# Second block of a transformer kernel: both heads of a pair in one attention unit, rotation by DMA instead of a matmul

## The chip, the cores and the metric

The kernel runs on one core of one Trainium2 chip. The metric is the device time of one execution in microseconds. Three runs of the kernel before gave 2832.24, 2833.23 and 2835.91 us; the median is 2833.23.

## What is computed

A first block of two layers (feed forward, a mixer with pooling, a Fourier part and differential attention, feed forward) and a second block of two layers. The change touches the second block alone:

```python
def hybrid_layer(x, mem, norm_g, w_in, w_out, mem_norm_g, w_mem_kv, qk_g):   # T = 512, D = 1024
    proj = rms_norm(x, norm_g) @ w_in
    a_q, a_k, a_v, a_g, b_q, b_k, b_v, b_g, m_q, m_g = split(proj)           # 6 + 6 + 4 heads of 64
    qa, ka = rope(rms_norm(heads(a_q), qk_g[0])), rope(rms_norm(heads(a_k), qk_g[1]))
    oa = moba_attention(qa, ka, heads(a_v))          # causal: T = 512 is two blocks, all of them kept
    qb, kb = rope(rms_norm(heads(b_q), qk_g[2])), rope(rms_norm(heads(b_k), qk_g[3]))
    ob = dilated_attention(qb, kb, heads(b_v))       # one softmax with a mask of log counts
    m_k, m_v = split(rms_norm(mem, mem_norm_g) @ w_mem_kv)                   # 256 memory rows
    om = memory_attention(rms_norm(heads(m_q), qk_g[4]), rms_norm(m_k, qk_g[5]), m_v)
    y = concat([oa * silu(a_g), ob * silu(b_g), om * silu(m_g)])
    return x + y @ w_out
```

rope turns a head's halves x1, x2 of 32 rows into x1 cos - x2 sin and x2 cos + x1 sin.

## The kernel before

**Precision.** Each float32 product is made of three matmuls of split operands (hi times hi, hi times lo, lo times hi), by `three` (L414 to L420). A weight panel is 128 x 2048 numbers: SyncE loads it into one of two raw buffers, ScalarE copies it to w_hi (`split`, two instructions of 1024 columns, L840), GpSimd subtracts the rest into w_lo (L410, four of 512 columns). Activations lie feature-major, features on partitions, the 512 tokens along the row.

**Groups.** A layer of the second block has eight groups. Group 0 is the memory's keys and values, group 1 the memory queries and gates, groups 2 to 7 one pair of heads each, with four chunks: queries, keys, values, gate. A chunk is 8 x 3 matmuls of 128 x 512, half of it 12.

**Stages.** `run_stages` goes through the layer in stages, and in each the attention of one group stands beside the projection (`producer`) of the next. The memory stage has 16 steps, every second one with half a chunk. Each pair stage has 8 steps with half a chunk each: five with a producer (groups 2 to 6 attend, 3 to 7 are projected), and a last one (group 7) beside which the output projection begins (`beside_last`, then `tail` and `project_out`).

**A unit** is one head and one block of 128 queries; its width is 256 for memory, and 128, 256, 384, 512 keys for blocks 0 to 3 of a pair. In step s each engine runs, in this order written by hand (`attention_step`):
- TensorE: scores of unit s (three matmuls on the 64 rows of the head, bank s % 2); transposes of unit s - 3 by the identity (L705, bank 2 + s % 2); after each fourth unit, a step later, the outputs of that head (`outputs`, in bank 5); in step 5 the transposes of the values (L717); then the producer's part: in steps 2 and 4 first the rotation and the mean of squares as plain float32 matmuls (L730, L731), then half a chunk in bank 4 (the gate in bank 7).
- VectorE: mask and maximum of unit s (L1452), negation; in step 7 the split of the next pair's queries and keys (qk_hi, qk_lo, L1438 and L1187 in `head_split`); scaling of unit s - 1 by the reciprocal sum (att, L1473); remainder of the transposed unit s - 3 (pt_lo); the gate product; the producer's part: in steps 3 and 5 mean and rotation (L1515 to L1528), in step 6 value, Newton steps and scaling (L1531, L1180, L1182, L1432).
- ScalarE: first the producer's part (copy and square of the chunk, L1029 and L1030, steps 2 and 4, and in step 4 a weight split); exp of unit s (L1056); copy of the transposed unit s - 3 (pt_hi, L1065); in step 5 the guesses of the reciprocal roots (L858), in step 7 a weight split and the gate's Silu (L1045). Silu, exp and root each load their table.

Engines are joined by counting semaphores: t_scores, t_max, t_exp, t_att, t_tr, t_thi, t_tlo for the links of a unit, t_o and t_y for outputs, hn_in, hn_mm, hn_ms, hn_rot, hn_guess, hn_out for queries and keys. TensorE starts a pair stage only after hn_out, that is, after qk_lo.

Of the kernel before, what the change touches and what calls it, by code (L numbers as in the profile page):

```python
# [71 lines left out]
C_ID, C_MEAN, C_HALF, C_HEAD, C_ROT = range(5)  # L72
NC = 5 * P + 1
# [22 lines left out]
UNITS2 = 64  # L96
PAIR_UNITS = 2 * TB


class Stage:  # L100
# [3 lines left out]
    def __init__(self, l, gi, branch):  # L104
        self.l, self.gi, self.branch = l, gi, branch
        self.memory = branch is None
        self.last = isinstance(gi, int) and gi == GROUPS - 1
        if self.memory:
            self.n, self.widths = 4 * TB, [256] * (4 * TB)
            self.u0, self.heads0 = UNITS2 * l, 16 * l  # L110
        else:
            self.n, self.widths = PAIR_UNITS, [P * (b + 1) for _ in range(2) for b in range(TB)]
            self.u0 = UNITS2 * l + 4 * TB + PAIR_UNITS * (gi - 2)
            self.heads0 = 16 * l + 4 + 2 * (gi - 2)
# [4 lines left out]
LAG_TR = 3  # L119
LAG_OUT = 4  # L120
LAG_GATE = 5
# [5 lines left out]
def lagged(here, before, s, lag):  # L127

    i = s - lag
    if i < 0:  # L130
        return (before, before.n + i) if before else None
    return (here, i) if here and i < here.n else None


def run_stages(l, fori, step, producer, last=None, tail=None):


    def stage(here, before, produce):
        for s in range(here.n if here else LAG_GATE + 1):
            if here and here.memory:  # L140
                step(here, before, s, produce, s // 2 if s % 2 == 0 else None)
            else:
                step(here, before, s, produce, s)
    memory = Stage(l, 1, None)
    stage(memory, None, producer(l, 2))
    pair = Stage(l, 2, 0)
    stage(pair, memory, producer(l, 3))
    for first, branch in ((3, 0), (5, 1)):
        with fori(0, 2) as j:
            pair = Stage(l, first + j, branch)  # L150
            stage(pair, Stage(l, first - 1 + j, branch), producer(l, first + 1 + j))
    pair = Stage(l, 7, 1)
    stage(pair, Stage(l, 6, 1), last)
    stage(None, pair, tail)


def shape_constants():
# [7 lines left out]
    rot = np.zeros((P, P))  # L165
    for m in range(P):
        if m % 64 < 32:
            rot[m + 32, m] = -1.0
        else:
            rot[m - 32, m] = 1.0  # L170
    consts[:, C_ROT * P:(C_ROT + 1) * P] = rot
# [14 lines left out]
    rope = np.stack([np.cos(ang).T[i % 32], np.sin(ang).T[i % 32]], 1)  # L186
# [18 lines left out]
def build(nc, x, mem, stream, vecs1, vecs2, final_g, lamv, consts, dist, masks, recip, rope, out):  # L205
    ctx = ExitStack()
    with ctx:  # L207
# [78 lines left out]
        vm_hi = sb("vm_hi", [P, 2, 2, 2, P], F32R, two)  # L286
        vm_lo = sb("vm_lo", [P, 2, 2, 2, P], F32R, two)
# [3 lines left out]
        pt_hi = sb("pt_hi", [P, TB, T], F32R, two)  # L291
        pt_lo = sb("pt_lo", [P, TB, T], F32R, two)
        rope_sb = sb("rope_sb", [P, 2, T], F32, two)
        mask = sb("mask", [P, 2, T], F32, two)
        prob2 = sb("prob2", [P, 2, T], F32, two)
        att2 = sb("att2", [P, 2, T], F32, two)
        xs = sb("xs", [P, 2, T], F32, two)
        qk_hi = sb("qk_hi", [P, 2, T], F32R, two)
        qk_lo = sb("qk_lo", [P, 2, T], F32R, two)
        two.close()  # L300
        mh_hi = pt_hi[:].rearrange("p a (b n) -> p (a b) n", b=2)
        mh_lo = pt_lo[:].rearrange("p a (b n) -> p (a b) n", b=2)
# [61 lines left out]
        hn_rot = sem("hn_rot")  # L364
        hn_guess = sem("hn_guess")
# [49 lines left out]
        def _(pe):  # L415
# [245 lines left out]

            def scores(stage, u):
                h, b = u // TB, u % TB
                r, c, w = slice(64 * (h % 2), 64 * (h % 2) + 64), slice(P * b, P * b + P), slice(0, stage.widths[u])
                if stage.memory:
                    k_split = km_hi[r, h // 2, w], km_lo[r, h // 2, w]
                else:
                    k_split = qk_hi[r, 1, w], qk_lo[r, 1, w]
                return three(ps[:, u % 2, w], qk_hi[r, h // 2, c], qk_lo[r, h // 2, c], *k_split, True, True)

            def outputs(stage, h):
                l, gi = stage.l, stage.gi
                if stage.memory:
                    if h == 2:
                        pe.wait_ge(t_y, 8 * l + 1)
                    for kb in range(2):
                        mm = three(ps[:, 5, :], vm_hi[:, kb, h // 2, h % 2, :], vm_lo[:, kb, h // 2, h % 2, :],
                                   pt_hi[:, kb, :], pt_lo[:, kb, :],
                                   h % 2 == 0 and kb == 0, h % 2 == 1 and kb == 1)
                else:  # L680
                    if h == 0:
                        pe.wait_ge(v_tlo, 7 * l + gi)
                    for kb in range(TB):
                        c = slice(P * kb, T)
                        mm = three(ps[:, 5, c], vp_hi[:, kb, h, :], vp_lo[:, kb, h, :],
                                   pt_hi[:, kb, c], pt_lo[:, kb, c],
                                   h == 0 and kb == 0, h == 1 and kb == TB - 1)
                mm.then_inc(t_o, 1)

            def attention_step(here, before, s, produce, part):  # L690
                if here:
                    if s == 0 and not here.memory:
                        pe.wait_ge(hn_out, GROUPS * here.l + here.gi + 1)
                    unit2 = lagged(here, before, s, 2)
                    if unit2:
                        pe.wait_ge(t_exp if unit2[0].memory else t_max, here.u0 + s - 1)
                    scores(here, s).then_inc(t_scores, 1)
                unit = lagged(here, before, s, LAG_TR)
                if unit:
                    stage, u = unit  # L700
                    pe.wait_ge(t_att, stage.u0 + u + 1)
                    if u >= 2 or not stage.memory:
                        pe.wait_ge(t_tlo, stage.u0 + u - 1)
                    for kb in range(stage.widths[u] // P):
                        mm = pe.transpose(ps[:, 2 + u % 2, P * kb:P * kb + P],  # L705
                                          att2[:, u % 2, P * kb:P * kb + P], const(C_ID))
                    mm.then_inc(t_tr, 1)
                unit = lagged(here, before, s, LAG_OUT)
                if unit and unit[1] % TB == TB - 1:
                    stage, u = unit  # L710
                    pe.wait_ge(t_tlo, stage.u0 + u + 1)
                    outputs(stage, u // TB)
                if here and not here.memory and s == 5:
                    pe.wait_ge(v_in, 7 * here.l + here.gi)
                    pe.wait_ge(t_y, 8 * here.l + here.gi)
# [4 lines left out]
                if produce and part is not None:  # L720
                    produce(part)

            def producer(l, gi):
# [3 lines left out]
                rot0 = 12 * l + 2 * (gi - 2)  # L727

                def rotate(j):
                    pe.matmul(ps[:, 6, :], const(C_ROT), xs[:, j, :], start=True, stop=True)  # L730
                    pe.matmul(ps[:, 7, :], const(C_HALF), sq[:, j, :], start=True, stop=True).then_inc(hn_mm, 1)  # L731

                def step(s):
                    if s > 7:
                        return
# [20 lines left out]
                    if s % 2:  # L756
                        mm.then_inc(panel_done if c % 2 else chunk_ready, 1)
                return step

            def stack2(l):  # L760
# [44 lines left out]
                def beside_last(s):  # L805
# [8 lines left out]
                run_stages(l, pe.Fori, attention_step, producer, beside_last, tail)  # L814
                project_out(p0 + 2 * GROUPS, 0, lambda i: pe.wait_ge(y_ready, 8 * l + i + 1), Y_ORDER,
                            (KB - 1, PAIR_UNITS - 2, 0, 0))
# [17 lines left out]
        def _(act):  # L834
# [212 lines left out]
            def attention_step(here, before, s, produce, part):  # L1047
                if produce and part is not None:
                    produce(part)
# [3 lines left out]
                if here:  # L1053
                    w = slice(0, here.widths[s])
                    act.wait_ge(t_max, here.u0 + s + 1)
                    act.activation(prob2[:, s % 2, w], ps[:, s % 2, w] if here.memory else prob2[:, s % 2, w],  # L1056
                                   ACT.Exp, bias=nmx[:, s % 2, 0:1], accum_out=ssum[:, s % 2, 0:1]).then_inc(t_exp, 1)
                unit = lagged(here, before, s, LAG_TR)
                if unit:
# [679 lines left out]
```

## Time and profile before

| | |
|---|---|
| three runs | 2832.24, 2833.23, 2835.91 us |
| profiled execution, its own time | 2830.71 us |
| its span | 2828.9 us |
| TensorE matmuls busy | 2607.4 us (92%) |
| VectorE busy | 1319.6 us (47%) |
| ScalarE busy | 1083.6 us (38%) |
| GpSimd busy | 1109.1 us (39%) |
| granted TensorE clock, mean | 0.957 |

A busy time is the sum over an engine's instructions; matmuls overlap their neighbours, so the length of one (0.39 us) is more than its distance to the next (0.23 us). Idle time in brackets in a row is the time before the instruction, and the arrow names what ended it. The second block takes the last 27% of the span.

### The profile page before, as it was taken

The numbers are of one execution on the slowest core, as the hardware profiler recorded it, in microseconds if no ns is written. First come the engines' busy times: TensorE is split into PE (matmuls) and PEld (weight loads), VectorE is DVE, ScalarE is ACT, GpSimd is POOL, SyncE is SP. The second block draws the span as 40 slices with busy tenths as digits, with TensorE's granted clock in tenths as the row PEclk, the third lists the DMA queues.
The fourth block names the chain that finished last, engine by engine and source line by source line (L and its number), as shares of the span: only waits on it lengthen the run. The fifth ranks groups of instructions, "written<-read, shape, count | busy, mean of one in ns | idle before, by whom it ended". The sixth has DMA issues, their size and how long they took to land.

```text
span 2828.9 us, 32377 instructions
## 1 busy us (share of the span) xinstructions
PE 2607.4 (92%) x11338; PEld 2055.2 (73%) x11338; DVE 1319.6 (47%) x2355; ACT 1083.6 (38%) x1594; POOL 1109.1 (39%) x828
## 2 busy tenths in 40 slices
PE   6999999679999999999997799999989997889988
PEld 5887887457887888878874578878756665756656
DVE  5544034645443044440346454430856666556563
ACT  4333133534332143331335343321545442545442
POOL 3544445214544445544452145454512222412222
PEclk9999999789999999999997899999989998999989
DMA  4222233102222222222331022223201111201111
GB/s 154 90 101 92 89 110 113 45 29 91 89 104 89 90 91 102 96 97 90 105 117 45 27 93 89 103 90 120 104 30 60 45 45 45 90 30 46 59 45 60
DMA packets 32858, 226.94 MB, mean 80 GB/s; under 512 B 4096, under 2 KB 4096, under 8 KB 6016
## 3 DMA queue, kind: packets, MB, share of 16 engines
q1 hardware_dynamic: 30816, 218.12, 21.6%
q10 hardware_dynamic: 1952, 7.61, 0.7%
q8 instruction: 58, 0.95, 0.1%
q14 instruction: 32, 0.26, 0.0%
HBM read 223.62 MB, written 2.10 MB: 80 GB/s over the span
## 4 chain that ended last, share of the span: by engine, by line
issue 63%; POOL 37%; POOLq 1%
POOL w_lo L410 37%; POOLq L404 0%; POOLq L408 0%; POOLq L207 0%; POOLq L410 0%; POOLq L1730 0%
## 5 line engine op out<-in xcount | busy, mean ns | idle before, releaser
L410 POOL TENSOR_TENSOR w_lo<-raw,w_hi 128x512 fp32r<-128x512 f32 x824 | 1108.9, 1377 | 1719.3 <-ACT w_hi L840 1718.9
L418 PE MATMUL ps<-h_hi,w_hi 128*128 128x512 f32 x2304 | 937.2, 407 | 32.0 <-POOL w_lo L410 11.2
L419 PE MATMUL ps<-h_lo,w_hi 128*128 128x512 f32 x2304 | 910.0, 395 | 0.0
L420 PE MATMUL ps<-h_hi,w_lo 128*128 128x512 f32 x2304 | 909.7, 395 | 0.0
L840 ACT ACTIVATE w_hi<-raw 128x1024 fp32r<-128x1024 f32 x412 | 413.3, 1052 | 827.6 <-PE ps L420 819.7
L418 PEld LDWEIGHTS ps<-h_hi,w_hi 128*128 128x128 f32 x2304 | 441.1, 191 | 136.0 <-issue 29.5
L419 PEld LDWEIGHTS ps<-h_lo,w_hi 128*128 128x128 f32 x2304 | 441.4, 192 | 97.7 <-issue 9.5
L420 PEld LDWEIGHTS ps<-h_hi,w_lo 128*128 128x128 f32 x2304 | 440.3, 191 | 95.2
L418 PE MATMUL ps<-hid_hi,w_hi 128*128 128x512 f32 x704 | 279.7, 397 | 7.5 <-DVE hid_lo L1187 7.5
L420 PE MATMUL ps<-hid_hi,w_lo 128*128 128x512 f32 x704 | 278.6, 396 | 0.0
L419 PE MATMUL ps<-hid_lo,w_hi 128*128 128x512 f32 x704 | 278.3, 395 | 0.0
L1240 DVE SCALAR_TENSOR_TENSOR x_sb<-ps,x_sb 128x512 f32<-128x512 f32 x64 | 43.7, 687 | 438.7 <-PE ps L420 438.7
L1259 DVE TENSOR_TENSOR sq<-hraw,sq 128x512 f32<-128x512 f32 x88 | 139.7, 1588 | 222.6 <-ACT hraw L927 222.6
L840 ACT ACT_TABLE_LOAD x42 | 53.9, 1283 | 320.2 <-PE ps L420 315.7
L418 PEld LDWEIGHTS ps<-hid_hi,w_hi 128*128 128x128 f32 x704 | 132.6, 188 | 41.1 <-DVE hid_lo L1187 9.2
L1255 DVE TENSOR_TENSOR hraw<-ps,guess 128x512 f32<-128x512 f32 x88 | 60.8, 691 | 213.2 <-PE ps L420 212.4
L420 PEld LDWEIGHTS ps<-hid_hi,w_lo 128*128 128x128 f32 x704 | 132.6, 188 | 32.9
L419 PEld LDWEIGHTS ps<-hid_lo,w_hi 128*128 128x128 f32 x704 | 132.4, 188 | 31.6
L1056 ACT ACTIVATE prob<-prob,nmx 128x128 f32<-128x128 f32 (+1 forms) x96 | 54.0, 563 | 204.4 <-DVE nmx L1456 204.0
L1187 DVE TENSOR_TENSOR pt_lo<-ps,pt_hi 128x256 fp32r<-128x256 f32 (+3 forms) x128 | 60.6, 474 | 127.6 <-ACT pt_hi L1065 127.6
L1261 DVE CAST hid_hi<-sq 128x512 f32 (+1 forms) x88 | 111.2, 1264 | 14.7 <-issue 14.5
L1187 DVE TENSOR_TENSOR hid_lo<-sq,hid_hi 128x512 f32 (+1 forms) x88 | 100.6, 1143 | 12.6 <-issue 0.2
(261 smaller groups left out, 2669.6 us busy)
## 6 DMA issues: line engine op xcount, KB each, us to landing
raw<-in_stream SPq DMA_DIRECT2D x206, 1024.0 KB, 4.9
x_sb<-in_x ACTq DMA_DIRECT2D x1, 2048.0 KB, 10.6
out_x<-x_sb SPq DMA_DIRECT2D x8, 256.0 KB, 2.7
mem_sb<-in_mem ACTq DMA_DIRECT2D x1, 1024.0 KB, 13.5
rec_sb<-in_recip ACTq DMA_DIRECT2D x2, 512.0 KB, 4.8
memn<-in_mem ACTq DMA_DIRECT2D x1, 1024.0 KB, 4.9
dist_sb<-in_dist ACTq DMA_DIRECT2D x2, 448.0 KB, 3.8
mask<-in_masks ACTq DMA_DIRECT2D x1, 512.0 KB, 5.9
```

The source lines that it names most:

```text
L410: ins = gp.tensor_tensor(w_lo[:, s, c], raw[:, s, c], w_hi[:, s, c].bitcast(F32), ALU.subtract)
L418: pe.matmul(dst, l_hi, r_hi, start=first, stop=False)
L419: pe.matmul(dst, l_hi, r_lo, start=False, stop=False)
L420: return pe.matmul(dst, l_lo, r_hi, start=False, stop=last)
L840: act.activation(w_hi[:, s, c], raw[:, s, c], ACT.Copy).then_inc(hi_split, 1)
L1056: act.activation(prob2[:, s % 2, w], ps[:, s % 2, w] if here.memory else prob2[:, s % 2, w], ACT.Exp, bias=nmx[:, s % 2, 0:1], accum_out=s ...
L1187: return dve.tensor_tensor(dst, src, hi.bitcast(F32), ALU.subtract)
L1240: dve.scalar_tensor_tensor(out=x_sb[:, m, :], in0=ps[:, m, :], scalar=scale, in1=x_sb[:, m, :], op0=ALU.mult, op1=ALU.add).then_inc(x_read ...
L1255: dve.tensor_tensor(hraw[:, e, :], ps[:, 2 * e, :], rstd, ALU.mult).then_inc(gate_in, 1)
L1259: dve.tensor_tensor(sq[:, e, :], hraw[:, e, :], sq[:, e, :], ALU.mult)
L1261: dve.tensor_copy(hid_hi[:, c, :], sq[:, e:e + 1, :])
```

## The change

`UNITS2` falls from 64 to 32 a layer. A unit is now both heads of a pair and one query block: the memory group has 8, each pair 4, and all stages have 8 steps, pair stages a unit in every second one (`every = 2`), written out without loops. Scores go by `paired`, head 0 to bank 0 and head 1 to bank 1, interleaved; the transposes of a pair unit fill banks 2 and 3, prob2 and att2 hold one unit. The lags are 1 for the scaling, 2 for the transposes, 3 for the outputs (both heads at once), 4 for the gate product. The rotation matmul is gone: ScalarE's queue issues four DMAs of 32 partitions that write xs, with its halves exchanged, to hraw, and the sign lies in the table. The mean matmul stands behind the half-chunk. The final-norm products of x_sb go to the odd steps of stages 2 and 3.

```diff
-LAG_TR = 3
-LAG_OUT = 4
-LAG_GATE = 5
+LAG_ATT = 1
+LAG_TR = 2
+LAG_OUT = 3
+LAG_Y = 4
...
+            def paired(dst, l_hi, l_lo, r_hi, r_lo, first, last):
+
+                for a, b, f, z in ((l_hi, r_hi, first, False), (l_hi, r_lo, False, False), (l_lo, r_hi, False, last)):
+                    for h in range(2):
+                        mm = pe.matmul(dst[h], a[h], b[h], start=f, stop=z)
+                return mm
...
+                    if u and stage.memory:
+                        pe.wait_ge(t_exp, stage.u0 + u)
+                    elif not stage.memory:
+                        pe.wait_ge(t_exp if u == 0 and before.memory else t_max, stage.u0 + u)
+                    scores(stage, u).then_inc(t_scores, 1)
+                unit = lagged(here, before, s, LAG_OUT)
+                if unit and ends_group(unit[1]):
+                    stage, u = unit
+                    pe.wait_ge(t_tlo, stage.u0 + u + 1)
...
-                    pe.matmul(ps[:, 6, :], const(C_ROT), xs[:, j, :], start=True, stop=True)
...
+                def turn(j):
+
+                    g = v2_all[:, bass.ds(NV2 * l + G_QK + 2 * gi + j, 1)]
+                    act.activation(xs[:, j, :], ps[:, 4, :], ACT.Copy, scale=g).then_inc(xs_ready, 1)
+                    act.activation(sq[:, j, :], ps[:, 4, :], ACT.Square).then_inc(hn_in, 1)
+                    act.wait_ge(xs_ready, rot0 + j + 1)
+                    if j == 1:
+                        act.wait_ge(hn_rot, rot0 + 1)
+                    for i in range(4):
+                        o, n = 32 * i, 32 * (i ^ 1)
+                        act.dma_start(hraw[o:o + 32, 1, :], xs[n:n + 32, j, :]).then_inc(turned, 16)
...
+                        dve.wait_ge(turned, 64 * (12 * l + 2 * (gi - 2) + j + 1))
                         dve.tensor_tensor(xs[:, j, :], xs[:, j, :], rope_sb[:, 0, :], ALU.mult)
-                        dve.tensor_tensor(hraw[:, 1, :], ps[:, 6, :], rope_sb[:, 1, :], ALU.mult)
+                        dve.tensor_tensor(hraw[:, 1, :], hraw[:, 1, :], rope_sb[:, 1, :], ALU.mult)
```

ScalarE in a pair stage, from step 4 to the end of step 7: xs and sq are copy and square of the keys, prob the exp, pt_hi the copy of the transposes, w_hi a weight split. Before:

```order
L1029 ACTIVATE xs<-ps,v_all 128x512
L1030 ACTIVATE sq<-ps 128x512
L837 ISA
L840 ACTIVATE w_hi<-raw 128x1024 x2
L1055 REGISTER_ALU
L1056 ACTIVATE prob,ssum<-prob,nmx 128x128
L1065 ACTIVATE pt_hi<-ps 128x2x128
```

In the changed kernel, the same place:

```order
L1113 ACTIVATE xs<-ps,v_all 128x512
L1114 ACTIVATE sq<-ps 128x512
L1120 DMA hraw<-xs 32x512 x4
L852 ACTIVATE w_hi<-raw 128x1024 x2
L1075 ACTIVATE prob,ssum<-prob,nmx 128x384 x2
L1089 ACTIVATE pt_hi<-ps 128x2x2x128
```

Four DMA issues now stand between the square and the weight split, and the exp and the copy behind it are those of two heads and of wider blocks.

VectorE at the end of a pair stage, steps 6 and 7: mx and nmx are the maximum, hraw the value, newt and guess the Newton steps. Before:

```order
L1187 TENSOR_TENSOR pt_lo<-ps,pt_hi 128x4x128
L1531 TENSOR_TENSOR hraw<-ps,scale 128x512
L1180 SCALAR_TENSOR_TENSOR newt<-ms,newt 128x1024
L1182 SCALAR_TENSOR_TENSOR guess<-newt,guess 128x1024
L1432 SCALAR_TENSOR_TENSOR xs<-xs,guess 128x512 x2
L1445 REGISTER_ALU
L1451 MEMSET tick 128x1
L1452 ISA prob,mx<-ps,mask 128x512
L1452 ISA mx 128x1
L1456 TENSOR_SCALAR nmx<-mx 128x1
L1438 CAST qk_hi<-xs 128x1024
L1187 TENSOR_TENSOR qk_lo<-xs,qk_hi 128x1024
```

In the changed kernel:

```order
L1490 ISA prob,mx<-ps,mask 128x512
L1490 ISA mx 128x1
L1493 TENSOR_SCALAR nmx<-mx 128x2
L1223 TENSOR_TENSOR pt_lo<-ps,pt_hi 128x2x3x128
L1569 TENSOR_TENSOR hraw<-ps,scale 128x512
L1216 SCALAR_TENSOR_TENSOR newt<-ms,newt 128x1024
L1218 SCALAR_TENSOR_TENSOR guess<-newt,guess 128x1024
L1468 SCALAR_TENSOR_TENSOR xs<-xs,guess 128x512 x2
L1474 CAST qk_hi<-xs 128x1024
L1223 TENSOR_TENSOR qk_lo<-xs,qk_hi 128x1024
L1511 RECIPROCAL rsum<-ssum 128x2
L1514 TENSOR_SCALAR att<-prob,rsum 128x512 x2
```

The maximum of the widest block moved from between xs and the split to ahead of the remainder, which is that of two heads; no unit stands in step 7.

## Rows read from the trace of the kernel before

**Rows 1.** Stretches: start:end, length, busy us (count) of each engine, clock, DMA.

```profile
2050.90:2114.75 63.85, 52.93 (x197) 35.83 (x197) 38.92 (x100) 24.52 (x57) 8.23 (x7) 0.85 0.09 33
2114.75:2336.96 222.21, 203.84 (x872) 147.49 (x871) 135.76 (x375) 112.88 (x208) 51.30 (x40) 0.96 0.13 48
2336.96:2385.96 49.00, 41.38 (x171) 30.77 (x172) 29.07 (x86) 14.21 (x34) 5.25 (x4) 0.79 0.06 22
2464.57:2523.03 58.46, 48.77 (x196) 33.49 (x196) 33.18 (x92) 24.52 (x57) 7.79 (x7) 0.91 0.10 37
2523.03:2743.70 220.67, 201.84 (x872) 145.45 (x872) 135.72 (x375) 112.78 (x208) 51.33 (x40) 0.97 0.13 48
2743.70:2791.05 47.35, 39.86 (x171) 29.70 (x172) 28.80 (x85) 14.10 (x34) 5.27 (x4) 0.82 0.06 23
```

**Rows 2.** Waits of TensorE from 2114 us on: us in total, times, longest.

```profile
PE ps L418 <- DVE qk_lo L1187: 26.8, 10, 3.1
```

**Rows 3.** First block's scores by tile k_hi, 552 to 554 us: ns, first and last start.

```profile
L418 PE MATMUL ps<-k_hi,q_hi x2: 791/792/792, 552.2 to 552.3; 64*128 64x512 f32 x2
```

**Rows 4.** TensorE in order of time, pair stage from 2159 us: start, length, line, operation.

```profile
2167.90 1.13 PE L730 MATMUL ps<-xs,cst 128*128 128x512 f32 x2
2168.86 1.02 PE L731 MATMUL ps<-sq,cst 128*128 128x512 f32 x2
...
2172.57 0.50 PE L418 MATMUL ps<-qk_hi 64*128 64x512 f32 x1
...
2173.55 0.48 PE L418 MATMUL ps<-pt_hi,vp_hi 128*128 128x512 f32 x1
...
2175.49 0.45 PE L418 MATMUL ps<-h_hi,w_hi 128*128 128x512 f32 x1
...
2178.41 0.33 PE L418 MATMUL ps<-qk_hi 64*128 64x128 f32 x1
```

**Rows 5.** VectorE in order of time, end of the same stage.

```profile
2188.75 0.68 DVE L1525 TENSOR_TENSOR xs<-xs,rope_sb 128x512 f32<-128x512 f32 x1
...
2190.72 0.55 DVE L1452 CUSTOM_DVE_ANT_0 prob<-ps,mask 128x384 f32<-128x384 f32 x1
...
2193.59 0.69 DVE L1187 TENSOR_TENSOR pt_lo<-ps,pt_hi 128x512 fp32r<-128x512 f32 x1 [1.54 <-ACT pt_hi L1065]
...
2198.98 0.69 DVE L1452 CUSTOM_DVE_ANT_0 prob<-ps,mask 128x512 f32<-128x512 f32 x1
...
2199.82 0.68 DVE L1438 CAST qk_hi<-xs 128x1024 fp32r<-128x1024 f32 x1
...
2201.96 1.47 DVE L1473 TENSOR_SCALAR att<-prob,rsum 128x384 f32<-128x384 f32 x1
```

**Rows 6.** ScalarE in order of time, the same stage.

```profile
2161.43 0.63 ACT L1045 ACTIVATE y<-y 128x512 f32<-128x512 f32 x1 [0.15 <-DVE y L1510]
2162.09 1.28 ACT L1056 ACT_TABLE_LOAD   x1
...
2178.62 0.69 ACT L1029 ACTIVATE xs<-ps,v_all 128x512 f32<-128x512 f32 x1 [2.65 <-PE ps L420]
...
2179.68 2.00 ACT L840 ACTIVATE w_hi<-raw 128x1024 fp32r<-128x1024 f32 x2
...
2192.37 0.62 ACT L1056 ACTIVATE prob<-prob,nmx 128x384 f32<-128x384 f32 x1
2192.99 0.58 ACT L1065 ACTIVATE pt_hi<-ps 128x512 fp32r<-128x512 f32 x1
```

**Rows 7.** A DMA issue on ScalarE's queue, and DMA issues by line: us to landing.

```profile
1973.07 0.45 ACTq L946 DMA_DIRECT2D mask<-in_masks  x1
...
out_x<-x_sb SPq DMA_DIRECT2D x8, 256.0 KB, 2.7
```

**Rows 8.** VectorE by tile: ns least, median, most; sq in the first block, qk_lo.

```profile
L1259 DVE TENSOR_TENSOR sq<-hraw,sq x88: 1476/1667/1823, 43.7 to 1883.5; 128x512 f32<-128x512 f32 x88
...
L1187 DVE TENSOR_TENSOR qk_lo<-xs,qk_hi x14: 1224/1225/2129, 2048.0 to 2742.4; 128x1024 fp32r<-128x1024 f32 x14
```

More of the change, by code:

```diff
@@ L129, in lagged, with ends_group, run_stages @@
     i = s - lag
[L130 to L154, printed above, removed]
+    stage = here if i >= 0 else before
+    i %= STEPS
+    if stage is None or s - lag >= STEPS or i % stage.every:
+        return None
+    return stage, i // stage.every
+def ends_group(u):
+    return u % TB == TB - 1
+def run_stages(l, step, producer, last=None, tail=None):
+    before = None
+    for gi in range(1, GROUPS):
+        here = Stage(l, gi, None if gi == 1 else (gi - 2) // 3)
+        produce = producer(l, gi + 1) if gi + 1 < GROUPS else last
+        for s in range(STEPS):
+            step(here, before, s, produce)
+        before = here
+    for s in range(LAG_Y):
+        step(None, before, s, tail)
 def shape_constants():
@@ L290, in build @@
         km_lo = sb("km_lo", [P, 2, 256], F32R, two)
[L291 to L296, printed above, removed]
+        pt_hi = sb("pt_hi", [P, 2, TB, T], F32R, two)
+        pt_lo = sb("pt_lo", [P, 2, TB, T], F32R, two)
         xs = sb("xs", [P, 2, T], F32, two)
@@ L665, in scores @@
                 if stage.memory:
-                    k_split = km_hi[r, h // 2, w], km_lo[r, h // 2, w]
-                else:
[L668 to L688, printed above, removed]
@@ L690, in attention_step @@
-            def attention_step(here, before, s, produce, part):
-                if here:
+                    q, k = [[t[r, u // TB, c] for r in rows] for t in (mq_hi, mq_lo)], (km_hi, km_lo)
+                    k = [[t[r, u // TB, w] for r in rows] for t in k]
+                else:
+                    q = [[t[r, 0, c] for r in rows] for t in (qk_hi, qk_lo)]
+                    k = [[t[r, 1, w] for r in rows] for t in (qk_hi, qk_lo)]
+                return paired([ps[:, h, w] for h in range(2)], *q, *k, True, True)
@@ new lines, in outputs @@
+            def outputs(stage, u):
+                kbs = 2 if stage.memory else TB
+                for h in range(2):
+                    for kb in range(kbs):
+                        if stage.memory:
+                            c, v = slice(0, T), (vm_hi[:, kb, u // TB, h, :], vm_lo[:, kb, u // TB, h, :])
+                        else:
+                            c, v = slice(P * kb, T), (vp_hi[:, kb, h, :], vp_lo[:, kb, h, :])
+                        mm = three(ps[:, 5, c], *v, pt_hi[:, h, kb, c], pt_lo[:, h, kb, c],
+                                   h == 0 and kb == 0, h == 1 and kb == kbs - 1)
+                return mm
@@ L692, in attention_step @@
+            def attention_step(here, before, s, produce):
+                unit = lagged(here, before, s, 0)
+                if unit:
+                    stage, u = unit
                     if s == 0 and not here.memory:
                         pe.wait_ge(hn_out, GROUPS * here.l + here.gi + 1)
[L694 to L697, printed above, removed]
+                    if u and stage.memory:
[5 more added lines that the diff above has]
+                if unit and ends_group(unit[1]):
+                    stage, u = unit
+                    pe.wait_ge(t_tlo, stage.u0 + u + 1)
+                    if not stage.memory:
+                        pe.wait_ge(v_tlo, 7 * stage.l + stage.gi)
+                    elif u >= TB:
+                        pe.wait_ge(t_y, stage.outs0 + 1)
+                    outputs(stage, u).then_inc(t_o, 1)
@@ L719, in attention_step @@
                     mm.then_inc(v_tr, 1)
-                if produce and part is not None:
-                    produce(part)
+                if produce:
+                    produce(s)
             def producer(l, gi):
```

248 lines of the change are left out of this document (134 added, 114 removed).

## The prediction

> **What bounds the kernel now.** I read the time by stage first, because the change only touches the two attention layers at the end [rows 1]. A layer's memory stage takes 63.85 and 58.46 us, its five pair stages with a producer take 222.21 and 220.67 us (44.3 each), and the last pair stage with the start of the output projection 49.00 and 47.35 us. In the five stages TensorE is busy 204 of 222 us: these are bound by TensorE. What it waits for is small and always the same: 26.8 us in ten waits for VectorE's qk_lo [rows 2], once a stage, when the next pair's queries and keys are not yet split. So two questions decide: how much TensorE work goes, and whether VectorE and ScalarE can follow when TensorE asks sooner. In the memory stage TensorE already idles (52.9 of 63.9 us), so there only the waits count.
>
> **TensorE work that goes.** The rotation matmul costs 0.96 us (2167.90 to 2168.86) [rows 4], twice a stage: 1.9 us. The scores of the two heads of a pair lie on different row halves. In the first block the program has three matmuls for one half and then three for the other, and the first matmuls of both halves start within 0.1 us of each other, with equal durations [rows 3]: the halves run at once. A pair of score units then costs what one costs now: 0.98 us at width 512 with its hand-over (2172.57 to 2173.55) [rows 4], and by columns some 0.5, 0.6, 0.8 for the narrower ones. Four of eight units and their hand-overs from and to the 128-row matmuls go: 3.3 us a stage, as an estimate. Together 5.2 of some 40 us a stage, 52 us over ten stages: that is the offer. Nothing else shrinks: four half-chunks and four more (2.75 each, 2.92 with hand-over), outputs 1.94 a head, means 0.9 [rows 4].
>
> **What the change puts in their place.** Scores use banks 0 and 1 for one unit, transposes banks 2 and 3 for one unit, prob2 and att2 hold one unit. Every link of softmax is now twice as long and the distance from scores to transposes falls from three steps to two. And rotation issues eight DMAs a stage on ScalarE's queue: one there took 0.45 us [rows 7], so some 1.7 us for four. What stands behind them on ScalarE, the weight split and the next exp, starts only then. Landing, 2.7 us for the nearest row, out_x [rows 7], is hidden: the DMAs leave 2.5 to 4 us before VectorE has the mean it needs as well.
>
> I walk one pair stage with the new orders, zero being TensorE's first scores:
> - 0 to 6.7. VectorE scales unit 3 of the pair before (0.9), then gate (0.6); ScalarE Silu 0.65, table 1.3 [rows 6], exp of unit 0 twice 0.4, copy of the 1024 columns of unit 3, 1.0; VectorE's remainder 1.2. Scores and transposes of unit 3 and a half-chunk keep TensorE until 4.6 (6 at the low clock), then it waits for that remainder, since both heads' outputs come now, in step 1. Before, they came in steps 3 and 7, with slack.
> - to 13.4: outputs 3.9, half-chunk 2.75. To 21.4: ScalarE's copy and square, half-chunk, mean, half-chunk (1.6 with its hand-overs [rows 6], then 2.75, 0.9, 2.75). All TensorE's.
> - to 28.0 on ScalarE: hand-over and copy 1.0, four DMA issues 1.7, weight split 2.0 [rows 6], exp of unit 2 twice 0.61, copy of unit 1 0.5.
> - to 36.0 on VectorE: remainder 0.7; scaling of unit 2 2.4, since GpSimd runs then and one scale of 384 columns takes 1.47 beside it (2201.96), the second being half free of it; v remainder 0.7; mean 0.6 and rotation 2.0 (2188.75 to 2190.72); maximum of unit 3 1.6 (two of 0.69 and their tails) [rows 5].
> - to 38.3: ScalarE exp twice 0.72, copy 0.8. To 46.1: VectorE remainder, value, Newton steps and scaling 5.2 (2193.59 to 2198.98, less a pause of 0.25) and 0.4 for the wider remainder, split 2.1 (2199.82 to 2201.96) [rows 5], then TensorE may start the next pair.
>
> TensorE is done at 38.4 and waits, 7.7 us instead of 2.6. One item comes on top. ScalarE now starts the second weight split as soon as TensorE is done, because no exp stands in step 7, so GpSimd's four subtractions (5.1 us a panel: 51.3 over ten panels [rows 1]) run from 39.7 to 44.9, beside VectorE's longest SBUF chain, not after it. An SBUF product of 512 columns takes 1476 to 1823 ns in the first block beside GpSimd [rows 8] and 0.68 alone [rows 5]; qk_lo took 2129 ns in one case and 1225 in the usual one [rows 8]. Between these two, about half of 5 us is lost: 2.4. A stage is 48.5.
>
> A page of the Trainium skill has a sharper rule (SBUF — State Buffer, Who interferes with whom): a VectorE operation with two SBUF inputs and a GpSimd one exclude each other for the whole instruction. The rows agree in direction and give 0.9 us more on each of three operations. If all four subtractions were each waited for in full, the rule would give 5.1 in place of 2.4; that is rival C.
>
> **Bounds for a stage.** Below: 46.1 if GpSimd costs nothing there, and 44.4 if the DMA issues cost nothing either (no row shows a cheaper one, so 0 is the end). Above: 51.2 with 5.1 for GpSimd, and 53 if the low clock after the long wait (0.79 in the last stage [rows 1]) stretches the outputs. I take 48.5.
>
> **Memory stage.** Eight units instead of sixteen. The walk: two half-chunks to 8.6 (low clock at the start as now); copy, square, four issues, exp, copy on ScalarE to 13.4; Silu of 1024 with two loads, exp and copy to 18.6; remainder, mean, rotation to 21.8; issues, split, exp, copy to 27.0; remainder and maximum 28.5; exp, copy, remainder to 31.3; mean, guesses, exp, copy to 37.0; remainder, Newton, maximum, split to 45.2. With 0.8 for the clock 46, against 63.85 and 58.46: a gain of 30.3. The rows behind it are the same durations [rows 4 to 6].
>
> **The rest.** The eight final-norm products of x_sb move from the memory stage (where VectorE had time) into pair stages 2 and 3 of layer 0: some 0.7 each, of which the four in steps 3 and 5 lie on the chain, +3. The first pair stage of a layer has only a memory group's outputs to wait for: -1.5 each. In the last stage nothing waits for qk_lo; y_ready from VectorE paces it (6 matmuls a step). The same walk gives 36.0 to the last scores' project and 50.4 to the end of the tail, against 49.00 and 47.35: +4.4. Zeroing of vm in the other half of pt between layers: +1. Unrolled loops save a few register instructions a stage; nothing waits for them.
>
> **Sum.** -30.3 + 10 x (48.5 - 44.3) = 42.1, + 3 - 3 + 4.4 + 1 = +17.2. The profiled execution is 2830.7 us with a span of 2828.9; it comes to 2848. The three runs' median, 2833.2, lies 2.5 above the profiled one: **2850 us**, 0.6% slower.
>
> The skill's page TensorEngine Tiling (PSUM Bottleneck) warns of this: tiling speeds the matmuls and not the evacuation of PSUM. Here VectorE's and ScalarE's chain behind the scores is not shortened at all, which is the walk's result.
>
> **Rivals.**
> A, the chain is 2 us shorter than walked (GpSimd hidden, 46.1): -7, so 2826. For it: qk_lo took its full 1225 in most stages [rows 8]. Against: that is since the split runs later there. The sign turns at a stage of 46.8.
> B, TensorE stays the bound, with the old wait of 2.6 and 35.9 of work: 38.5 a stage, -58 - 30 + 5 = -83, 2750. It needs all links hidden; against it, VectorE waits 1.54 for ScalarE's copy even now at step 6 [rows 5], and the link doubles. The offer of 52 us with the waits as they are, and the memory gain, lies on the same side: 2756.
> C, GpSimd's lock and the low clock in full: 52 a stage, +35 more, 2885.
> D, the row halves do not run at once in this form: TensorE +2.6 a stage, of it 1 on the path: 2860.
>
> **Chances.** Forecast with 47.2 to 50 a stage (2837 to 2865) 0.45; A with 45 to 47.2 (2815 to 2837) 0.22; B 0.1; C 0.14; D 0.04; between B and A 0.05. Range 2800 to 2888. A difference under 0.2% (5.7 us) can't be told by a measurement of this kernel. Faster: B, the gap, and half of A, 0.26. Same: 0.16, the rest of A and the forecast's edge. Slower 0.58.
>
> **What would show it.** Right: TensorE's wait for qk_lo 6 to 11 us once in each of the ten stages; a wait for pt_lo before the outputs in step 1; scores of both heads starting within 0.1 us; GpSimd beside newt, guess and xs, which take over 1.5 us; memory stages of 44 to 48. Wrong: stages under 46 with waits for qk_lo under 4 us, DMA issues of well under 0.4 us, or VectorE waiting for turned.

## The result and the profile after

The changed kernel takes 2872.7 us (median, 2871.0 to 2874.7), the kernel before 2832.9 (2832.2 to 2835.9) in the same comparison. The ratio is 1.0139, with a 95% interval of 1.0121 to 1.0156: 39.8 us slower. The forecast was 17.2 slower, so the loss is more than twice what was forecast. The profiled execution has a span of 2869.1 us, 40.2 above the 2828.9 before, and the time is accounted for below against spans.

Stretches of the changed kernel, with the columns of [rows 1]: memory stage, first, second and last but one pair stage, the five together, last stage with tail, all of layer 0; then memory stage, five pair stages and last stage with tail of layer 1.

```profile
2050.60:2097.78 47.18, 39.23 (x185) 28.81 (x186) 28.54 (x57) 23.93 (x52) 7.75 (x7) 0.92 0.18 56
2097.78:2145.79 48.01, 34.94 (x160) 25.95 (x161) 33.90 (x69) 24.76 (x41) 17.53 (x12) 0.87 0.19 63
2145.79:2198.71 52.92, 38.39 (x173) 29.17 (x174) 31.14 (x64) 21.82 (x37) 11.91 (x8) 0.85 0.14 46
2299.04:2348.86 49.82, 36.84 (x173) 28.22 (x173) 28.29 (x60) 21.83 (x37) 12.48 (x8) 0.88 0.16 53
2097.78:2348.86 251.08, 184.16 (x849) 139.73 (x849) 150.64 (x310) 112.06 (x189) 66.90 (x44) 0.87 0.17 54
2348.86:2411.27 62.41, 46.11 (x201) 36.40 (x201) 34.31 (x87) 14.76 (x29) 5.03 (x5) 0.80 0.03 12
...
2481.41:2528.45 47.04, 38.62 (x184) 28.39 (x184) 28.69 (x57) 23.92 (x52) 7.74 (x7) 0.93 0.17 56
2528.45:2776.71 248.26, 183.18 (x849) 139.06 (x849) 145.30 (x302) 112.08 (x189) 67.39 (x44) 0.87 0.18 55
2776.71:2838.18 61.47, 44.21 (x200) 34.98 (x201) 26.85 (x69) 14.64 (x29) 5.03 (x5) 0.83 0.03 12
```

Against [rows 1]: the memory stages give 28.1 us (63.85 and 58.46 became 47.18 and 47.04), the ten pair stages cost 56.5 (442.9 became 499.3). The last stages end here at TensorE's wait for the second output panel, which stood at 2394.30 and 2798.88 before; to there they took 57.34 and 55.18, so they cost 11.4. Everything else is +0.5.

GpSimd shows the first oddity: eight subtractions a stage kept it busy for 10.3 us (51.30 for 40) before, and keep it busy for 12.5 now, in the fifth stage's row.

TensorE's wait for qk_lo and ScalarE's pauses in the second block of the changed kernel (in total, times, longest); the first row answers to [rows 2], where it had 26.8 us:

```profile
PE ps L668 <- DVE qk_lo L1223: 115.2, 12, 11.2
ACT w_hi L852 <- issue: 35.8, 12, 4.8
ACT prob L1075 <- issue: 26.1, 12, 2.6
```

"issue" is what the profile writes where it sees no releaser. Here it is mostly time in which ScalarE hands out DMAs; the two longest, 4.8 us each in the memory stages, also hold a wait for VectorE (see rotmm below).

### The profile page after: what moved, and what is told of

It reads as the page before. It is cut to its first block, busy times and chain, and to the rows that moved or that the text cites. A ratio compares the mean times of both kernels' runs of the same rounds, so it can differ in the third digit from the quotient of the medians.

```text
span 2869.1 us, 31223 instructions
## 1 busy us (share of the span) xinstructions
PE 2545.6 (89%) x11290; PEld 2033.6 (71%) x11290; DVE 1314.1 (46%) x2101; ACT 1074.0 (37%) x1530; POOL 1129.0 (39%) x828
## 4 chain that ended last, share of the span: by engine, by line
issue 63%; POOL 37%; POOLq 1%
POOL w_lo L412 37%; POOLq L406 0%; POOLq L410 0%; POOLq L202 0%; POOLq L412 0%; POOLq L1771 0%
## 5 line engine op out<-in xcount | busy, mean ns | idle before, releaser
L412 POOL TENSOR_TENSOR w_lo<-raw,w_hi 128x512 fp32r<-128x512 f32 x824 | 1128.8, 1401 | 1739.6 <-ACT w_hi L852 1739.3
L1223 DVE TENSOR_TENSOR pt_lo<-ps,pt_hi 128x256 fp32r<-128x256 f32 (+2 forms) x68 | 52.1, 768 | 179.3 <-ACT pt_hi L1089 179.2
L668 PE MATMUL ps<-qk_hi 64*128 64x128 f32 (+3 forms) x96 | 22.1, 456 | 115.2 <-DVE qk_lo L1223 115.2
L1297 DVE CAST hid_hi<-sq 128x512 f32 (+1 forms) x88 | 111.3, 1265 | 14.7 <-issue 14.4
## 6 DMA issues: line engine op xcount, KB each, us to landing
x_sb<-in_x ACTq DMA_DIRECT2D x1, 2048.0 KB, 10.3
```

Source lines behind the costliest of these rows:

```text
L412: ins = gp.tensor_tensor(w_lo[:, s, c], raw[:, s, c], w_hi[:, s, c].bitcast(F32), ALU.subtract)
L668: mm = pe.matmul(dst[h], a[h], b[h], start=f, stop=z)
L1223: return dve.tensor_tensor(dst, src, hi.bitcast(F32), ALU.subtract)
L1297: dve.tensor_copy(hid_hi[:, c, :], sq[:, e:e + 1, :])
```

## Where the time of a pair stage goes

The pair stage from 2299.04 us (TensorE's first scores) to 2348.86, in order of time. First TensorE:

```profile
2299.04 0.47 PE L668 MATMUL ps<-qk_hi 64*128 64x128 f32 x2 [11.19 <-DVE qk_lo L1223]
...
2328.78 0.50 PE L668 MATMUL ps<-qk_hi 64*128 64x512 f32 x2
2329.12 0.39 PE L668 MATMUL ps<-qk_lo,qk_hi 64*128 64x512 f32 x2
2329.35 0.39 PE L668 MATMUL ps<-qk_hi,qk_lo 64*128 64x512 f32 x2
```

x2 is the matmul of head 0 and that of head 1 in one row: both together take 0.39 us, which is what one takes, and the next such pair starts 0.23 us later, the distance of single matmuls. The row halves do run at once. ScalarE, steps 4 and 6:

```profile
2321.13 0.59 ACT L1114 ACTIVATE sq<-ps 128x512 f32<-128x512 f32 x1
2321.64 2.44 ACTq L1120 DMA_DIRECT2D hraw<-xs  x4
2324.13 2.01 ACT L852 ACTIVATE w_hi<-raw 128x1024 fp32r<-128x1024 f32 x2 [2.41 <-issue]
2326.04 0.60 ACT L1075 ACTIVATE prob<-prob,nmx 128x384 f32<-128x384 f32 x1
...
2327.24 0.58 ACT L1089 ACTIVATE pt_hi<-ps 128x512 fp32r<-128x512 f32 x1
...
2337.71 2.00 ACT L852 ACTIVATE w_hi<-raw 128x1024 fp32r<-128x1024 f32 x2
```

VectorE in the same stage, steps 4 to 7:

```profile
2327.85 0.69 DVE L1223 TENSOR_TENSOR pt_lo<-ps,pt_hi 128x512 fp32r<-128x512 f32 x1 [5.08 <-ACT pt_hi L1089]
...
2328.69 1.93 DVE L1514 TENSOR_SCALAR att<-prob,rsum 128x384 f32<-128x384 f32 x2
...
2338.54 0.68 DVE L1569 TENSOR_TENSOR hraw<-ps,scale 128x512 f32<-128x512 f32 x1
2339.14 2.06 DVE L1216 SCALAR_TENSOR_TENSOR newt<-ms,newt 128x1024 f32<-128x1024 f32 x1
2341.27 2.13 DVE L1218 SCALAR_TENSOR_TENSOR guess<-newt,guess 128x1024 f32<-128x1024 f32 x1
2343.47 3.27 DVE L1468 SCALAR_TENSOR_TENSOR xs<-xs,guess 128x512 f32<-128x512 f32 x2
2346.81 0.69 DVE L1474 CAST qk_hi<-xs 128x1024 fp32r<-128x1024 f32 x1
2347.58 1.22 DVE L1223 TENSOR_TENSOR qk_lo<-xs,qk_hi 128x1024 fp32r<-128x1024 f32 x1
```

GpSimd in step 7 of that stage, four subtractions in one row:

```profile
2338.84 7.35 POOL L412 TENSOR_TENSOR w_lo<-raw,w_hi 128x512 fp32r<-128x512 f32 x4 [8.44 <-ACT w_hi L852]
```

The chain reads from the bottom: TensorE waits 11.19 us for qk_lo; VectorE is never idle from 2337.66 on; newt, guess and xs run while GpSimd does (2338.84 to 2346.19), and both are slow: GpSimd's four subtractions take 1.27, 2.24, 2.24 and 1.71 us one by one, where those of step 4 take 1.28 to 1.38. VectorE had waited 5.08 us for ScalarE's copy, and ScalarE had spent 2.44 us on four issues ahead of the split, the exp and that copy. A DMA lands 2.1 us after its issue (median of 96), and VectorE waits for it nowhere.

The walk of the prediction against this stage, in us after the first scores:

| point | walked | measured |
|---|---|---|
| remainder of unit 3 done (VectorE) | 6.7 | 6.6 |
| copy of the keys begins (ScalarE) | 21.4 | 21.5 |
| copy of unit 1's transposes done | 28.0 | 28.8 |
| maximum of unit 3 done | 36.0 | 36.3 |
| copy of unit 2's transposes done | 38.3 | 38.6 |
| qk_lo done | 46.1 + 2.4 = 48.5 | 49.8 |

Two prices were low: an issue takes 0.61 us, not 0.45, and GpSimd beside VectorE's last stretch costs more than 2.4 us.

## Experiments

### late7: GpSimd's second run moved off VectorE's last stretch

> The changed kernel, with ScalarE's second weight split of a group taken out of the end of step 7 and put into step 1 of the next pair stage (not before the last stage, which needs the panel at once). So GpSimd's four subtractions no longer run beside newt, guess and xs. Theory 1, GpSimd beside VectorE's SBUF chain costs it: in the changed kernel these lasted 2.06, 2.13 and 3.27 us beside GpSimd and 1.22, 1.23 and 1.29 where it was idle, 3.7 us a stage; ten stage ends: -37, 2836 us, waits for qk_lo of 7.5 instead of 11.2. Theory 2, the length of these operations is their own or TensorE's clock sets the stage: 2872, waits unchanged. Theory 3, the overlap only moves, to the operations of step 1 and 2: in between, 2855.

The first part of the edit stands in `gates_out`, at the end of step 7; the second in step 1, behind the copy.

```diff
-                act.wait_ge(panel_done, p + 2)
-                split(p + 3, 1)
+                if beside.gi == GROUPS - 2:
+                    act.wait_ge(panel_done, p + 2)
+                    split(p + 3, 1)
...
+                if here and s == 1 and 2 <= here.gi < GROUPS - 1:
+                    p = BASE2 + LAYER2_PANELS * here.l + 2 * here.gi
+                    act.wait_ge(panel_done, p + 2)
+                    split(p + 3, 1)
```

2839.4 us, ratio to the kernel before 1.0033 (1.0018 to 1.0047); its span is 31.6 below the changed kernel's. Of VectorE and GpSimd, pair stage from 2237.7 us:

```profile
2244.47 2.23 DVE L1519 TENSOR_SCALAR att<-prob,rsum 128x128 f32<-128x128 f32 x2
...
2277.82 1.22 DVE L1221 SCALAR_TENSOR_TENSOR newt<-ms,newt 128x1024 f32<-128x1024 f32 x1
2279.11 1.23 DVE L1223 SCALAR_TENSOR_TENSOR guess<-newt,guess 128x1024 f32<-128x1024 f32 x1
2280.41 1.29 DVE L1473 SCALAR_TENSOR_TENSOR xs<-xs,guess 128x512 f32<-128x512 f32 x2
```

Theory 1 holds: in this stage the three fall from 7.46 to 3.74 us and the stage from 49.8 to 46.1 (2237.72 to 2283.83). The ten pair stages together take 466.5 us instead of 499.3. The overlap has only moved, to the scalings of unit 0 (2.23 us instead of 0.48), but there TensorE has outputs to do, and the stage is shorter by all that the three gave up. The stage ahead of the last one, where the split was left in step 7, kept its wait of 11.2 us.

### nolow: GpSimd taken out

> The changed kernel, but in the second block GpSimd subtracts only 8 of each 512 columns: most of the low parts of the weights are left out. ScalarE's splits stay where they are, so all that goes is GpSimd's work beside VectorE. Theory 1: -3.7 a stage from newt, guess and xs, and the scalings of unit 2 (1.94 us each beside GpSimd) fall to about 0.7, -2.4: pair stages of 43.7 instead of 49.9, memory stages 4 less, some -65 in all, 2808. Theory 2 (GpSimd is no matter): stages of 49.9, 2872.

The kernel leaves out most of the low parts of the second block's weights, so it shows a cost and is no candidate. One execution: 2798.5 us, a span of 2796.6. Pair stages take 44.9 us (2228.84 to 2273.72, 2273.72 to 2318.66), 4.9 less. VectorE, same stretch:

```profile
2258.45 0.75 DVE L1524 TENSOR_SCALAR att<-prob,rsum 128x384 f32<-128x384 f32 x2
...
2267.72 1.21 DVE L1226 SCALAR_TENSOR_TENSOR newt<-ms,newt 128x1024 f32<-128x1024 f32 x1
```

3.7 of the 4.9 are newt, guess and xs, 1.2 the scalings of unit 2 (1.93 to 0.75). That is more than the rotation by DMA costs a pair stage (1.7, rotmm below). It is not a comparison with the kernel before, which pays for GpSimd too: one scaling of 384 columns takes 1.47 us there [rows 5]. The expectation of 43.7 counted 2.4 for the scalings; the two are one row of 1.93 us, not 1.93 each.

### rotmm: the rotation back to a matmul

> The changed kernel, with the rotation as a matmul again, behind the half-chunk and ahead of the mean: the DMA part of the change alone undone. Theory 1, the DMA issues lie on the chain: in step 4 ScalarE loses four issues of 0.61, 2.4 us, TensorE gets 0.96 on its stretch of the chain (step 2): -1.5 a pair stage, -15; memory stages -3 each: 2852. Theory 2, the issues are hidden and only TensorE's time counts: +1 to +2 a stage, 2885.

2844.6 us, ratio 1.0051 (1.0034 to 1.0067); the span is 27.3 below the changed kernel's, against 21 expected. Pair stages of 48.15 us (2701.86 to 2750.01) where the expectation had 48.4; over all ten 1.7 less each. Memory stages of 42.7 and 42.2 us, 4.5 and 4.8 less, where it had 3 less. Theory 1 holds, and the DMA half of the change costs 27 of the 40 us by spans (25 by the two ratios).

In the memory stage the issues aren't all of it. Second rotation of layer 1, in the changed kernel and then in rotmm, whose stages begin at 2481.41 and 2467.74:

```profile
2500.95 0.61 ACT L1114 ACTIVATE sq<-ps 128x512 f32<-128x512 f32 x1
2503.09 0.69 DVE L1566 TENSOR_TENSOR xs<-xs,hraw 128x512 f32<-128x512 f32 x1
2503.87 2.44 ACTq L1120 DMA_DIRECT2D hraw<-xs  x4
2506.36 2.00 ACT L852 ACTIVATE w_hi<-raw 128x1024 fp32r<-128x1024 f32 x2 [4.80 <-issue]
...
2486.87 0.59 ACT L1117 ACTIVATE sq<-ps 128x512 f32<-128x512 f32 x1
2487.34 2.01 ACT L855 ACTIVATE w_hi<-raw 128x1024 fp32r<-128x1024 f32 x2
```

At the square the changed kernel is only 0.4 us behind (0.1 in layer 0), so the first four issues cost next to nothing. At the weight split it is 5.35 behind, and at the exp after it 4.65 (4.3 in layer 0): ScalarE waits 2.3 us (from the end of the square, 2501.56) before its second four issues, which take 2.44. What it waits for is hn_rot: both rotations write the same half of hraw, so the second may overwrite it only after VectorE has added the first, which ends at 2503.78. In layer 0 it is the same, 2.3 us, and in the pair stage above some 0.4: there the issue starts 0.51 us after the square does, and 0.13 after it in step 2. No run gave the second rotation a place of its own.

### mem8: the memory stage alone, on the kernel before

> The kernel before, with only the memory stage changed: eight steps with both heads of a pair in a unit, rotation matmuls and pair stages as before; the x_sb products lie in steps 0, 1, 2 and 4 of the memory stage and of the first pair stage of layer 0. Theory 1, the memory stage's gain is that of paired units and does not need the DMAs: memory stages of 44 to 47 instead of 63.85 and 58.46, pair stages 44.3 as before, 2806. Theory 2, half of it comes from the rotation by DMA or is given back at the hand-over to pair units: 2820.

Of each pair of lags the first is that of a pair stage; the second part of the diff is from `scores`.

```diff
-LAG_TR = 3
-LAG_OUT = 4
-LAG_GATE = 5
+LAG_ATT = 1, 1
+LAG_TR = 3, 2
+LAG_OUT = 4, 3
+LAG_GATE = 5, 4
...
+                if stage.memory:
+                    rows, c, w = [slice(64 * i, 64 * i + 64) for i in range(2)], slice(P * b, P * b + P), slice(0, 256)
+                    q = [[t[r, h, c] for r in rows] for t in (qk_hi, qk_lo)]
+                    k = [[t[r, h, w] for r in rows] for t in (km_hi, km_lo)]
+                    return paired([ps[:, i, w] for i in range(2)], *q, *k)
```

2798.6 us, ratio 0.9889 (0.9873 to 0.9906): faster than the kernel before, as theory 1 says and, by the median, by 7 us more. Stretches of mem8: memory stage, first pair stage, the other four, layer 1:

```profile
2444.97:2488.35 43.38, 38.71 (x189) 28.06 (x189) 29.59 (x57) 24.08 (x52) 7.97 (x7) 0.96 0.14 49
2488.35:2536.29 47.94, 43.14 (x176) 30.75 (x176) 28.98 (x78) 22.75 (x42) 10.27 (x9) 0.93 0.13 44
2536.29:2714.20 177.91, 163.48 (x704) 118.35 (x705) 109.75 (x300) 89.51 (x165) 41.28 (x32) 0.96 0.14 48
```

The memory stage falls from 58.46 to 43.4 us (and from 63.85 to 43.9). Some of it comes back: the first pair stage takes 47.9 in both layers, where it took 44.4 and 42.8 in the kernel before. TensorE does the outputs of two memory heads in it, twelve matmuls instead of six, and waits 1.7 us for VectorE's xs before the second rotation. The last stages, whose order wasn't changed, took 54.1 and 53.3 us instead of 57.3 and 55.2, at a granted clock of 0.86 and 0.87 instead of 0.81 and 0.85; these 5 us are part of the gain, and no run shows whether they belong to the edit.

### late7_late4: the first split also behind the exp

> late7, and in step 4 ScalarE's weight split (2.0 us) also stands behind the exp and the copy, not ahead of them. Theory 1, ScalarE's stretch of the chain in step 4 sets the stage, so what stands ahead of the exp counts in full: -2 a stage against late7, 12 stages, -20 to -24: 2817. Theory 2, GpSimd, which now starts 2.5 us later, lands on vp_lo, ms and the rotation instead of on the scalings of unit 2, and gives it back: 2835 to 2839.

The edit moves `split(p + 2, 0)` of step 4 from the end of `turn(1)` to behind the copy of the transposes. 2841.0 us, ratio 1.0021 (1.0009 to 1.0032), where late7 has 1.0033 (1.0018 to 1.0047): not told apart. Theory 2 holds. VectorE waits 3.19 us for the copy instead of 5.08, and the 1.9 us come back soon after, in the rotation:

```profile
2267.36 0.69 DVE L1229 TENSOR_TENSOR pt_lo<-ps,pt_hi 128x512 fp32r<-128x512 f32 x1 [3.19 <-ACT pt_hi L1090]
...
2271.18 1.76 DVE L1569 TENSOR_TENSOR xs<-xs,rope_sb 128x512 f32<-128x512 f32 x1
2272.86 1.79 DVE L1570 TENSOR_TENSOR hraw<-hraw,rope_sb 128x512 f32<-128x512 f32 x1
2274.73 0.69 DVE L1572 TENSOR_TENSOR xs<-xs,hraw 128x512 f32<-128x512 f32 x1
```

In late7 the two products took 0.68 us each in the same step.

### late7_late4_rotmm: the paired kernel with all three mended

> late7_late4 with the rotation as a matmul. Alone that gave -28. Theory 1, the four issues of step 4 lie on the same chain whatever stands behind them: -1.7 a pair stage and -3 a memory stage again, so 25 less than late7_late4, 2792: the paired units would then beat the kernel before. Theory 2, once both splits are out of the way TensorE becomes the bound and its 1.9 us of rotation count: within 5 of late7_late4, 2815.

2822.2 us, ratio 0.9956 (0.9942 to 0.9971), its span 20.4 below late7_late4's. Between the two theories, nearer the first. Stages of 44.75 us (2634.89 to 2679.64) with TensorE still waiting 6.0 for qk_lo: even so mended, a paired stage takes no less than the 44.5 of mem8, and the two stages ahead of the last ones, where the split stayed in step 7, still take 48.6. The 12 us won over the kernel before are less than the memory stage alone brings.

### rotdma: the DMA rotation alone, on the kernel before

> The kernel before with the rotation by DMA alone; everything else as it was. Theory 1, TensorE bounds these stages, so 1.92 us less for it in each of twelve stages come off: -23, 2808. Theory 2, ScalarE's four issues of 0.61 delay the exp and the copy of step 4 and with them VectorE's queue, whose qk_lo TensorE already waits for: the wait grows from 2.6 to 5 us and eats the gain: 2835.

2821.2 us, ratio 0.9955 (0.9938 to 0.9972); the span is 9.3 lower (the spans are those of one execution each; the medians differ by 14.8, 8 to 18 by the interval). Neither theory holds in full. Waits of TensorE in the second block:

```profile
PE ps L414 <- DVE qk_lo L1193: 26.8, 10, 3.0
PE ps L726 <- ACT sq L1084: 18.7, 17, 3.1
PE ps L713 <- DVE y L1498: 9.5, 10, 1.0
```

The wait for qk_lo is 26.8 us, to the digit that of [rows 2], and the one for the square is 18.7 where it was 17.9: the issues delay neither. Of the 1.92 us of matmul that go from a stage, 0.9 turn into a new wait, for VectorE's product of y, once in each of ten stages. So one and the same edit gives 9 us by spans (13 by the ratio) where TensorE sets the pace in the pair stages, and costs 27 (25) where the chain over ScalarE does.

### mem8_pairdma, mem8_splitfirst, mem8_both: past both kernels

> mem8, with the rotation by DMA in the five pair stages only; the memory stage keeps its matmuls; the mean stands behind the half-chunk where the rotation goes by DMA. Theory 1, by rotdma the DMA is worth about 0.7 us a pair stage where TensorE sets the pace (43.85 instead of 44.5), so -7 against mem8: 2791. Theory 2, with the mean later VectorE's step 5 and the root guesses slip 2.8 us and the wait for qk_lo grows: 2800 or more.

> mem8, with the split of the next pair's queries and keys ahead of the mask and maximum in step 7 on VectorE. Theory 1, what stands ahead of qk_lo on VectorE there (0.69, two short ones and the negation, 0.85 us) is on the path, since TensorE waits 2.65 for qk_lo in each stage: waits of 1.8, 12 stages, -9: 2790. Theory 2, TensorE's wait is set elsewhere or the exp that now starts 2.1 us later takes it back: 2799.

> mem8_pairdma and mem8_splitfirst together. If both gains are real and on one path they add: 2783. If VectorE is then the one that TensorE waits for all the time, only one of them counts: 2790.

mem8_pairdma: 2792.2 us, ratio **0.9858** (0.9842 to 0.9875), the lowest here; its interval just touches that of mem8. Theory 1: the last four pair stages of layer 1 take 174.0 us where mem8 has 177.9, and the wait for qk_lo stays at 2.67.

```profile
2534.95:2708.99 174.04, 153.99 (x689) 112.66 (x689) 109.15 (x300) 89.88 (x166) 41.25 (x32) 0.98 0.19 61
```

mem8_splitfirst: 2805.7 us, ratio 0.9904 (0.9887 to 0.9920), by the intervals not told apart from mem8. The edit did what it says, the wait for qk_lo fell from 2.65 to 1.69 us, but no time came of it. Four stages of layer 0 gained 2.3 us together, those of layer 1 none, and the last stage went from 53.3 to 57.3 us (and from 54.1 to 58.9 in layer 0) with the clock at 0.82 instead of 0.87; TensorE waits there 3.72 us for a pt_lo instead of 2.89. Part of that is not the edit: mem8_pairdma, whose last stages are those of mem8, has 57.3 us at a clock of 0.81 in layer 0 and 53.2 at 0.87 in layer 1. The memory stages lost 1.2 us each: they now end with TensorE waiting 4.2 us for an exp, since the maximum stands behind the split, instead of 3.1 for qk_lo. That is theory 2's late exp. mem8_both: 2800.8 us, 0.9890 (0.9873 to 0.9906): above mem8_pairdma by the medians, so the two don't add.

### Sum of the parts

By spans, with what is paired along the side and the rotation on top:

| | rotation by matmul | by DMA |
|---|---|---|
| nothing paired | 2828.9 (before) | 2819.6 (rotdma) |
| memory stage paired | 2796.0 (mem8) | 2790.7 (mem8_pairdma, DMA in pair stages only) |
| all paired | 2841.8 (rotmm) | 2869.1 (after) |

Pairing the memory stage brings 33 us (5 of them in the last stages, see mem8), pairing the pair stages costs 46, and DMA then costs 27 more. The 46 hold all that rotmm has beyond mem8: the longer links, GpSimd beside VectorE, the later mean and the last stages. Of these late7 shows GpSimd's part in step 7 alone, on the changed kernel: 32 us by spans.

## Why the prediction was right in sign and too small

**What bounds the kernel: right.** Stages that TensorE filled (203.84 of 222.21 us) became stages of a chain through ScalarE and VectorE (184.16 of 251.08), with one wait of 9.6 to 11.2 us for qk_lo in each stage but the two first pair stages, 3.1 us there. The row halves run at once and the DMAs land in time, as predicted, and neither shortens a pair stage.

**The pair stage, 48.5 walked, 49.8 measured: three mis-sized terms.** The four issues were priced at 1.7 us from the one row of 0.45 us [rows 7]; they take 2.44, +0.7. "Between these two, about half of 5 us is lost: 2.4" is the step that failed most: late7 and nolow both put GpSimd's cost beside VectorE's last stretch at 3.7, +1.3, which is 13 us over ten stages and the largest part of the miss. The mechanism was right; the size was a guess between two values. The 0.9 us per operation that the prediction read from its rows was nearer: newt, guess and the two of xs are four operations, not three, and lost 0.84, 0.90 and twice 0.99. The scaling of unit 2 was taken at 2.4 and is 1.93, -0.5; a few tenths lie in the links. Over ten stages +14.4, with the x_sb products and the first stages, which the sum held at zero together. The stages came out within the forecast's own range for them (47.2 to 50, measured 49.9 on average); the time (2872.7 against 2837 to 2865) did not, because of the last stages.

On the rule named there (the Trainium skill, SBUF — State Buffer, Who interferes with whom): the traces agree in kind. VectorE's three lose 3.7 us and GpSimd, at 7.35 us for what takes 5.1 in step 4, loses 2.2, as if each waited for the other's current instruction in turn. Neither pays the full 5.1 that I drew from the rule. The page also counts a VectorE cast or tensor_scalar, which has one input, among those that can contend, in the modes that use both ports; the scalings (1.93 against 0.75) and the cast of qk_hi in rotmm (1.60 against 0.69) agree.

**Memory stage, 46 walked, 47.1 measured.** +2.2 over two stages. The walk put both blocks of four issues on the chain, at 1.7 us each. By rotmm and the rows there the first costs 0.4 us or less, and the second takes 2.44 and has a wait of 2.3 for hn_rot ahead of it that the walk didn't have. Together they leave the stage 4.3 and 4.65 us behind instead of 3.4: near the right number, partly by another cause.

**Last stage and tail, +4.4 forecast, +11.4 measured: the largest miss for its size.** This is the other term that was mis-sized, 7.0 us. The walk put one pacing item there, y_ready, and only 4.4 us for both layers. TensorE's waits in the last stage of layer 1 are four:

```profile
2783.36 0.80 PE L420 MATMUL ps<-pt_hi,vp_hi 128*128 128x512 f32 x1 [3.65 <-DVE pt_lo L1223]
2795.35 0.50 PE L420 MATMUL ps<-h_hi,w_hi 128*128 128x512 f32 x1 [3.09 <-DVE h_lo L1223]
2804.42 0.50 PE L420 MATMUL ps<-h_hi,w_hi 128*128 128x512 f32 x1 [2.80 <-DVE h_lo L1223]
2813.26 0.79 PE L420 MATMUL ps<-h_hi,w_hi 128*128 128x512 f32 x1 [4.10 <-DVE h_lo L1223]
```

They add up to 13.6 us. In the kernel before the same stage waited 7.4, and the difference is the 6.3 us that it grew by (55.18 to 61.47). TensorE is as busy as before (44.21 and 44.22 us), so it is the waits and not the clock. Three of the four are for h_lo, the split of y, so the item was the right one. It stands behind the attention's links in VectorE's order, and those links got longer; that this order is the cause is read from the traces, no run changed it. With +0.5 for the rest instead of +1 the misses add up: 14.4 + 2.2 + 7.0 - 0.5 = 23.1, against 40.2 - 17.2 = 23.0.

**The rivals.** A (a shorter chain, 2826) and B (TensorE stays the bound, 2750) are out; A's condition, GpSimd costing nothing, is nolow, whose stages take 44.9 where A had 46.1. C had the lock in the right direction but too high with 52 a stage. D is out by the rows of the scores. Of the signs named as right, one did not come: TensorE nowhere waits for pt_lo before the outputs of step 1 in the pair stage shown, since its half-chunk lasts until 2305.73 and the remainder is done at 2305.64. It does so in the last stages (3.65 us). The point at which the sign turns was put at stages of 46.8; late7's average 46.65 and it is still 0.33% slower, mainly because the last stages' loss was set too small.

## What to carry to other kernels

An edit is worth what the engine that sets the pace saves, and the same edit changes sign with that engine: the rotation by DMA gains 9 to 15 us beside TensorE-bound stages and loses 25 to 27 on a chain through the engine that issues it. Part of that loss can be a buffer: where a DMA writes what was read before, its issuer waits for the reader, and all that stands behind it waits as well. Units twice as large paid here only where TensorE idled around the hand-overs (the memory stage, 15 to 20 us each); in the pair stages, which TensorE filled, they lengthened every link of the chain and shortened the distance that hid it, and even with three mends a stage took 44.75 us against 44.5. Before moving a VectorE stretch, look whether GpSimd runs at that moment, and put GpSimd where nobody waits for VectorE.

## What the runs showed of the hardware

- Four DMA issues of 32 partitions from SBUF to SBUF keep ScalarE 2.44 us in most blocks, 0.61 each (median of 96; least 0.51, most 1.56). In the trace of before the issues on the same queue lay between 0.35 and 0.60.
- Beside GpSimd's subtraction VectorE's products, casts and scalings out of SBUF take 1.7 to 4.6 times as long in the rows above (newt 1.22 to 2.06; two scalings of 128 columns 0.48 to 2.23), while a remainder that reads PSUM keeps its time (pt_lo, 0.69 at 2327.85 beside GpSimd).
- The slowdown is mutual: GpSimd's four subtractions take 5.1 us in step 4, beside VectorE's two scalings, and 7.35 beside newt, guess and xs.
- Two matmuls on different row halves take the time of one, in the interleaved form too (0.39 us for 512 columns, both heads).
